# A two-block transformer forward pass in fp32: seams between stages rearranged, with rooms of their own for two splits, square root tables loaded ahead, and weight splits placed beside the tile reads that free them

## The reference, cut to what matters

```python
# first block
h = rmsnorm(x, norm_mix_g); p, q, k, v = split(h @ w_in)
pool_out = multiscale_pool(p); attn_out = diff_attention(rope(q), rope(k), v)
x = x + concat(pool_out, attn_out) @ w_o                       # stages proj1, wo
u = causal_dwconv(rmsnorm(x, norm_ffn_g) @ w_up)               # up1, 5632 wide
gate, val = split(u); x = x + (silu(gate) * val) @ w_down      # down1
x = rmsnorm(x, norm_final_g)
# second block
h = h + 0.5 * rms_norm(swiglu(rms_norm(h, ffn1_pre_g)), ffn1_post_g)      # up2, down2
u = rms_norm(h, mix_pre_g); proj = u @ w_in                               # proj2
y_a = sparse_latent_attention(proj); y_b = rms_norm(hgrn2(proj)) * silu(g_h)
merged = sigmoid(gate_a + b_gate[:D]) * (y_a @ w_br_a) \
       + sigmoid(gate_b + b_gate[D:]) * (y_b @ w_br_b)                    # branch
h = h + rms_norm(merged @ w_out, mix_post_g)                              # out
h = h + 0.5 * rms_norm(swiglu(rms_norm(h, ffn2_pre_g)), ffn2_post_g)      # up3, down3
ple_gate = sigmoid(rms_norm(h, ple_pre_g) @ w_ple_gate)                   # ple
h = h + rms_norm(ple_gate * (p @ w_ple_proj), ple_post_g)                 # pproj
```

## Time and profile before

| | |
|---|---|
| median of 3 runs | 2042.51 us (2041.75 to 2043.58) |
| profiled execution | 2042.38 us |
| its span | 2040.6 us |
| PE busy | 1855.1 us, 91% |
| DVE busy | 1169.4 us, 57% |
| ACT busy | 648.9 us, 32% |
| POOL busy | 201.3 us, 10% |
| DMA | 180.61 MB, mean 89 GB/s |

### The profile page before, as it was taken

One profiled execution on the slowest core, in us unless ns is written; L12 is line 12 of the kernel. 1 busy time (PEld: TensorE's weight loads), 2 busy tenths in 40 slices (PEclk: granted clock), 3 DMA queues, 4 the chain that ended last, 5 costly groups with the idle time before them and its releaser, 6 DMA issues.

```text
span 2040.6 us, 23459 instructions
## 1 busy us (share of the span) xinstructions
PE 1855.1 (91%) x8230; PEld 1481.6 (73%) x8230; DVE 1169.4 (57%) x1775; ACT 648.9 (32%) x954; POOL 201.3 (10%) x150
## 2 busy tenths in 40 slices
PE   5987999999999999999899989867778999999986
PEld 4665777777887888888677766656556788888864
DVE  6447568888534655532534786577663755552256
ACT  4333322222223222222323335443443422222243
POOL 2221000000000000000033344243000000000000
PEclk9888999999999999999899999978899999999988
DMA  3421222223322222332222332311242232232212
GB/s 136 82 67 38 83 73 93 93 93 104 100 95 78 86 100 95 98 112 95 67 83 73 121 127 63 131 40 32 72 134 83 73 103 93 96 118 96 91 50 74
DMA packets 55340, 180.61 MB, mean 89 GB/s; under 512 B 6216, under 2 KB 6984, under 8 KB 55272
## 3 DMA queue, kind: packets, MB, share of 16 engines
q1 hardware_dynamic: 43200, 157.07, 23.3%
q10 hardware_dynamic: 12072, 22.67, 4.0%
HBM read 167.65 MB, written 12.06 MB: 88 GB/s over the span
## 4 chain that ended last, share of the span: by engine, by line
PE 68%; DVE 20%; issue 6%; DMA 3%; ACT 2%; DVEq 1%; POOL 1%; ACTq 0%; SPq 0%; POOLq 0%
PE bank L713 17%; PE bank L715 16%; PE bank L714 16%; PE bank L735 2%; PE bank L736 2%; PE bank L737 2%; PE bank L794 2%; PE bank L795 2%; PE bank L796 2%; DMA raw<-in_w_proj 1%; DVE sq L1930 1%; PE bank L774 1%; DVE chunk L1751 1%; PE bank L1063 1%; DVE score L2079 1%
## 5 line engine op out<-in xcount | busy, mean ns | idle before, releaser
L1124 ACT ACTIVATE w_hi<-raw 128x1024 fp32r<-128x1024 f32 (+2 forms) x281 | 305.3, 1088 | 787.8 <-PE bank L715 703.3
L713 PE MATMUL bank<-a_hi,w_hi 128*128 128x512 f32 x1312 | 520.4, 397 | 25.2 <-DVE w_lo L1658 17.4
L714 PE MATMUL bank<-a_lo,w_hi 128*128 128x512 f32 x1312 | 513.7, 392 | 0.0
L715 PE MATMUL bank<-a_hi,w_lo 128*128 128x512 f32 x1312 | 513.6, 391 | 0.0
L1658 DVE TENSOR_TENSOR w_lo<-raw,w_hi 128x1024 fp32r<-128x1024 f32 (+2 forms) x219 | 279.7, 1281 | 267.1 <-ACT w_hi L1124 257.9
L713 PEld LDWEIGHTS bank<-a_hi,w_hi 128*128 128x128 f32 x1312 | 247.8, 189 | 96.0 <-issue 25.1
L715 PEld LDWEIGHTS bank<-a_hi,w_lo 128*128 128x128 f32 x1312 | 248.0, 189 | 52.4
L714 PEld LDWEIGHTS bank<-a_lo,w_hi 128*128 128x128 f32 x1312 | 248.1, 189 | 51.4 <-issue 1.0
L625 POOL TENSOR_TENSOR w_lo<-raw,w_hi 128x1024 fp32r<-128x1024 f32 x54 | 130.0, 2410 | 1106.6 <-ACT w_hi L1124 1106.6
L714 PE MATMUL bank<-h_lo,w_hi 128*128 128x512 f32 x568 | 221.1, 389 | 0.0
L715 PE MATMUL bank<-h_hi,w_lo 128*128 128x512 f32 x568 | 221.1, 389 | 0.0
(11 more groups left out here) (272 smaller groups left out, 2155.5 us busy)
## 6 DMA issues: line engine op xcount, KB each, us to landing
raw<-in_w_up SPq DMA_DIRECT2D x132, 512.0 KB, 3.3
...
```

The costliest lines, as they stand in the source:

```text
L713: mm(dst[:, :], wh, hi[:, k, :], start=(first and c == 0), stop=False)
L714: mm(dst[:, :], wh, lo[:, k, :], start=False, stop=False)
L715: step = mm(dst[:, :], wl, hi[:, k, :], start=False, stop=(last and c == n - 1))
L1124: fn(w_hi[:, slot, 0:size], raw[:, slot, 0:size], ACT.Copy).then_inc(unit_high, 1)
```

## The change

1. **Rooms.** wo's input gets its own `mix_hi` and `mix_lo`, so that `a_hi` and `a_lo` are free while wo runs. The split of x for up1 is made inside wo's tile loop, by ACT and by DVE. `sum_x("norm2")` moves from ahead of up1's first three tiles to behind them. pproj's input gets `p_split`.
2. **Root tables.** `load_root_table()`, a square root of one column, stands in ACT's queue at six places: at the end of the attention, after up2's silus, ahead of the branch stage, ahead of out, after up3's silus, and behind the last sigmoid of ple.
3. **Last square on PE.** For post1, postmix and plepost PE sums the sum of seven squares, then the eighth square onto it (16 products of one column), and DVE doesn't add the eighth.
4. **`add_branch`.** The first chunk takes its factor from PSUM, and the copy to `rstd` comes after the first `x`. `units` places two splits of ple's units within it.
5. **End.** post2's sum goes ahead of pproj's third tile and its spread ahead of the fifth; ACT's root, high parts, copies of pproj and split for ple are interleaved.
6. **Up stages.** In up1, up2 and up3 the split of unit 5 stands one tile earlier (up1: at the read of tile 1; up2 and up3: behind the first `val`).
7. **Branch.** The split of the unit that takes a tile's slot stands right behind the tile's read, no longer both behind `h_lo`.

The core of the diff:

```diff
             def sum_x(name):
+                stat_bank_free(name)
+                if name in LAST_ON_PE:
+                    q = square_at(name, DC - 1)
+                    pe.wait_ge(sum_added, q)
+                    sum_columns(sum_sq, stop=False)
+                    pe.wait_ge(sq_ready, q + 1)
+                    sum_columns(sq[:, q % 2, :], start=False).then_inc(total_ready, 1)
+                    return
                 pe.wait_ge(sum_added, square_at(name, DC - 1) + 1)
-                stat_bank_free(name)
                 sum_columns(sum_sq).then_inc(total_ready, 1)
 
...
-            first_three("wo", "mix1", spread_after=(1, 2, 3, 4))
+            first_three("wo", "mix1", mix_hi, mix_lo, spread_after=(1, 2, 3, 4))
             for i in range(3, DC):
-                project("wo", i)
-            hidden("up1", "norm2", AUX["pool", len(WINDOWS) - 1] + 1, summed=True)
+                project("wo", i, None, mix_hi, mix_lo)
+            hidden("up1", "norm2", AUX["pool", len(WINDOWS) - 1] + 1)
...
             for i in range(DC):
                 dst, u = tile_bank("pproj", i), UNIT["pproj"][0] + i // 4
+                if i == 2:
+                    sum_x("post2")
+                if i == 4:
+                    spread("post2")
...
+            def load_root_table():
+                fn(small[:, 60:61], prm("eps"), ACT.Sqrt)
...
                 if a == ATT_STEPS:
-                    highs("mix1", 0, 4)
+                    load_root_table()
+                    highs("mix1", 0, 4, mix_hi)
             unit_high_part(UNIT["wo"][0] + 3)
             take_root("head", P, HEADS * QB)
-            highs("mix1", 4, 4)
+            highs("mix1", 4, 4, mix_hi)
             for k in range(DC):
                 if k == DC - 1:
                     last_tile_finished("wo")
                 else:
                     tile_finished("wo", k)
+                wait(tile_read("wo", k))
+                scaled_high("norm_ffn_g", k)
                 square("norm2", k, x[:, k, :], tile_read("wo", k))
             unit_high_part(UNIT["up1"][0] + 3)
-            for k in range(DC):
-                scaled_high("norm_ffn_g", k)
             take_root("norm2", D)
...
             silus("up2", 1)
+            load_root_table()
             keep_branch("down2", "post1")
             take_root("post1", D)
...
             load_gates(1)
 
+            load_root_table()
             for t in range(4):
                 act.wait_ge(chunk_ready, SPLIT["y"] + t + 1)
                 fn(a_hi[:, t, :], ya[:, t, :], ACT.Copy).then_inc(hi_ready, 1)
...
             unit_high_part(UNIT["out"][0] + 3)
+            load_root_table()
             keep_branch("out", "postmix")
             take_root("postmix", D)
             scaled_highs("pre2", "ffn2_pre_g", 2 * DC, "up3")
             silus("up3", 2)
+            load_root_table()
 
             for c in range(2):
                 act.dma_start(pe_in[:, c, :], ins["pt"][c]).then_inc(p_loaded, 16)
-            highs("p", 0, 2)
+            highs("p", 0, 2, p_split)
             keep_branch("down3", "post2")
-            for i in range(DC):
+
+            def keep_pproj(i):
+
                 if i % 4 == 3:
                     units_done(UNIT["pproj"][0] + i // 4 + 1)
                 else:
                     act.wait_ge(head_ready, 2 * HEADS + DSA_HEADS + i - i // 4 + 1)
                 fn(p_proj[:, i, :], tile_bank("pproj", i)[:, :], ACT.Copy).then_inc(tile_sem("pproj", i), 1)
+
+            keep_pproj(0)
+            keep_pproj(1)
             take_root("post2", D)
-            scaled_highs("plepre", "ple_pre_g", 3 * DC, "ple")
+            unit_high_part(UNIT["ple"][0] + 1)
+            for i in (2, 3, 4):
+                keep_pproj(i)
+            for k in range(DC):
+                act.wait_ge(x_ready, 3 * DC + k + 1)
+                scaled_high("ple_pre_g", k)
+                if k < 3:
+                    keep_pproj(5 + k)
+                square("plepre", k, x[:, k, :], (x_ready, 3 * DC + k + 1))
+                if k < 2:
+                    unit_high_part(UNIT["ple"][0] + 2 + k)
+            take_root("plepre", D)
+            for n in range(2):
+                units_done(UNIT["ple"][0] + n + 1)
...
+                if i == DC - 1:
+                    load_root_table()
                 if i:
                     square("plepost", i - 1, p_proj[:, i - 1, :], (y_ready, i))
             take_root("plepost", D)
...
@@ -1739,23 +1794,30 @@
                         add_square(folded_to, k)
                     late_splits(stage, k)
 
-            def add_branch(name, g, src, last_read, signal, before, square_stage=None, split=None):
-
-                rsqrt(name)
+            def add_branch(name, g, src, last_read, signal, before, square_stage=None, split=None, units={}):
+
+                invert(name)
+                make_diagonal()
+                dve.wait_ge(spread_ready, STAT[name] + 1)
                 for k in range(DC + 1):
                     if k < DC:
                         if last_read is not None:
                             wait(last_read(k))
                         if k >= 2:
                             dve.wait_ge(signal, before + k - 1)
-                        step(v.scalar_tensor_tensor(chunk[:, k % 2, :], src[:, k, :], prm(g, k), rstd[:, :],
+                        factor = rstd if k else stat_bank
+                        step(v.scalar_tensor_tensor(chunk[:, k % 2, :], src[:, k, :], prm(g, k), factor[:, :],
                                                     ALU.mult, ALU.mult))
                         v.tensor_tensor(x[:, k, :], x[:, k, :], chunk[:, k % 2, :], ALU.add).then_inc(signal, 1)
+                    if k == 0:
+                        take_rstd(name)
                     if k and square_stage:
                         add_square(square_stage, k - 1)
                     if k and split:
                         scaled_low(split[0], split[1], k - 1)
                         add_square(split[0], k - 1)
+                    if k in units:
+                        split_unit(units[k])
...
                         dve.wait_ge(tile_sem("up1", tile), TILE["up1", tile][1] + 1 + it)
                         if i >= skip:
                             split_unit(first + 4 * turn + i + 3, it, 4)
+                        if skip and i == 1:
+                            split_unit(first + 5)
...
                         v.tensor_tensor(val[:, :], bank[u][:, :], rstd[:, :], ALU.mult).then_inc(bank_free[u], 1)
                         dve.wait_ge(bank_free[u], u_uses + 1 + it)
+                        if skip and j == 0:
+                            split_unit(u0 + 5)
...
-                    add_square(square_stage, k)
+                    if k < DC - 1 or square_stage not in LAST_ON_PE:
+                        add_square(square_stage, k)
...
                     wait(tile_read("branch", 2 * m + n))
+                    if m or n:
+                        split_unit(UNIT["branch"][0] + 2 * m + n + 3)
                 slot_free(c)
                 v.tensor_tensor(chunk[:, c % 2, :], gated[:, 0, :], gated[:, 1, :], ALU.add).then_inc(
                     chunk_ready, 1)
@@ -2270,8 +2337,6 @@
                     scale_gates(m + 1)
                 made(c)
                 low(c, h_lo[:, m, :], h_hi[:, m, :])
-                for u in (2 * m + 3, 2 * m + 4) if m else (4,):
-                    split_unit(UNIT["branch"][0] + u)
...
             branch_kept("down3", "post2")
-            for i in (1, 2):
-                split_unit(UNIT["ple"][0] + i)
             add_branch("post2", "ffn2_post_g", y, lambda k: tile_read("down3", k), x_ready, 3 * DC,
-                       split=("plepre", "ple_pre_g"))
+                       split=("plepre", "ple_pre_g"), units={0: UNIT["ple"][0] + 1, 2: UNIT["ple"][0] + 2})
```

60 lines of the change are left out of this document (36 added, 24 removed).

## The result

The changed kernel takes **2029.26 us** (median of 4 runs, 2027.11 to 2031.31) against 2043.05 (4 runs, 2041.75 to 2044.62): a ratio of 0.9933, 95% interval 0.9921 to 0.9945. It is faster by 13.8 us, where 20.6 was forecast, and lies just above the range. Its profiled execution is the slowest of the four, 2031.31 us with a span of 2029.4, so the two profiles differ by 11.2 us only.

A forecast was written before the change was run, and what follows sets the result against it. TensorE, busy 1855.1 of 2040.6 us, bounds the kernel; gains come only from 174 us idle and low-clock stretches. Terms sum to 20.6 us, taking the profiled 2042.4 to 2021.8 us, range 2015.5 to 2029.

The forecast's parts named there:

- the seam from wo to up1: End of wo to up1's first three tiles: they end 2.4 us earlier, bounds 1 and 3.5.
- the last seam: Behind ple: new table load delays the square and TensorE sums twice, a loss of 0.7 us, bounds -1.6 and +0.7.
- The branch stage's period: Branch stage: pairs of tiles 6.0 us apart instead of 7.09; with an earlier start +7.9 us, bounds 2.6 and 9.0.
- the table load ahead of it: Ahead of the branch stage: root table load and dummy root delay the high parts of ya, a loss of 1.5 us.
- the two seams with the eighth square on TensorE: Seams of down2 (post1) and out (postmix): one add saved, spread perhaps at full clock, +1.3 us each.
- pproj and ple: The end: post2's sum and spread hidden within pproj, ple starts 4.8 us earlier, +6.5 us in all.
- I take it to go with the gap: 1.7 more: up2, unit 5: half-clock stretch vanishes with the 1.86 us wait, adding 1.7 for +3.4 us; bounds 1.7 and 3.5.
- Rival 1: Branch stage: gates keep the period near 7.09 us, only the earlier start is won, 2.6 for 7.9; 2027 us, chance 0.15.
- rival 3: Table loads on the path stop their queue for twice their 1.28 us row, 2.6 us more; 2024.4 us, chance 0.08.
- the slower one: Up stages: early split of unit 5 shifts their phase, the 1.86 us wait returns each round; 2062 us, chance 0.02.
- Rival 5: Waits only move to the next unit in up2, and at the end; 2028 us, chance 0.08.
- Rival 2: Seams do better than bounded: full-clock spreads, wo's seam, hidden load, no last-seam loss, 4.3 us more; 2017.5 us, chance 0.22.

The follow-up runs named there:

- experiment 1: Changed kernel with mix_lo, the low part of wo's input, moved up by 32 bytes: 2026.02 us, ratio 0.9926.
- experiments 2 and 3: Kernel before with a_lo 32 bytes higher: 2061.34 us; changed kernel with mix_lo or mix_hi moved: 2027.91, 2028.48 us; both moved, plus up1's early low part: 2019.65 us.
- experiment 4: Changed kernel with mix_lo 96 bytes up and the low part of up1's unit 2 made before the wait for wo's last tile: 2020.22 us.
- experiment 6: Changed kernel with plepost's root table load and second sum undone: 2026.79 us; with only the second sum undone: 2025.53 us.
- experiment 8: Changed kernel with unit 5's split and high part in up2 and up3 back where they were: 2027.14 us.

## Why the prediction was wrong

**What failed.** Two terms of the sum were mis-sized, the seam from wo to up1 (0.3 for +2.4) and the last seam (-2.8 for -0.7), and the stretches between the seams were put at nothing, where they took 3.5 us back in this profile. Of the 20.6 forecast the two profiles show 11.2; these three make up 7.7 of the 9.4 that are missing, small parts the rest.

**Direction and most terms held.** The branch stage's period (5.95 for the 6.0 forecast), its gain (7.4 for 7.9), the table load ahead of it (-1.4 for -1.5), the two seams with the eighth square on TensorE (0.9 each for 1.3; the spreads stayed at half clock in this profile), pproj and ple (6.2 for 6.5; ple starts 17.24 us after pproj for 21.70, 4.5 for the 4.8 forecast) and the zeros of up1, up3, down3 and of the other loads came as worked out. In other runs the spread of one of the two seams ran at full clock (1.12 us in experiment 1's) and its seam took 9.13 for 10.96 before, a gain of 1.8, the upper bound. The table load at the attention's end (192.6 to 193.9 us) lies in ScalarE's wait for VectorE, which lasts to 195.9.

**"wo to up1: +2.4" gave 0.3.** The start of up1's tiles was right, 1.8 of the 2.0. What was not seen is that a room of its own has a place of its own: wo went from 0.680 to 0.700 us for three matmuls, -0.9 (experiments 2 and 3). I had checked what the new rooms overlap and not how fast they are read. Then, the stretch at half clock that began in the gap reached further into up1's first tiles (to 263.2, 5.8 us in, for 261.4, 4.9 us in), and they took 18.9 us for 18.5, where I had counted on 0.4 less. And the term asked which chain ends the wait, but not whether its last member had to stand there: it didn't, and 3.7 us lay in it (experiment 4).

**"The last seam: -0.7" was -2.8.** The wait for the squares grew by 0.2, where next to nothing was forecast, but the sums cost 3.55 us for 1.05: sixteen products at half clock. The term that was mis-sized is the second sum, which I had costed at 0.95, from the row of before, which happened to fall into full clock. The load costs 0.9 of the 2.8, the second sum 1.0, and 0.8 is the first sum at half clock (experiment 6). Even by its own terms, a start 0.03 later and 0.95 more of sum, the forecast would have been -1.0 and not -0.7.

**The clock, and one execution.** up2's "I take it to go with the gap: 1.7 more" came out (3.3 for 3.4) by luck: with the gap there the stretch stayed away in two executions of three (experiment 8). The edit is worth 1.7 and not 3.4; the profiled execution of before had a stretch there by chance. Stretches that were put at nothing show how large such chance is: over the runs based on the changed kernel start to wo's first took 195.9 to 198.8 us in a profile, and proj2 to the wait ahead of the branch stage 434.7 to 440.8, and here they took 3.5 of the gain back (1.8 and 1.7). Not all of that is the clock: 0.7 of the 1.8 were there before TensorE's first matmul (19.40 us for 18.68), and how the rest divides is not shown. I had set a sum of single seams against one execution as if the rest stood still. The 174 us of idle time that the prediction starts from are 185.5 by the earlier trace rows; no term was worked out from them.

**The range** of 2015.5 to 2029.0 took in each rival alone but not three terms short at once. Rival 1 (the gates bind), rival 3 (a load that costs twice its row) and the slower one are refuted: 5.95, 1.37 and 2029.26. Rival 5 (the wait moves to the next unit in up2 and at the end as well) did not come: no such wait is left in up2, and the end gained 6.2. In up1 it does move, as forecast, for the earlier trace rows:

```profile
295.97 0.50 PE L721 MATMUL bank<-a_hi,w_hi 128*128 128x512 f32 x1 [1.12 <-DVE w_lo L1711]
```

TensorE waits one unit later, 1.12 for 3.10, and the stage is no shorter. Rival 2 (all seams at their best) did not come either.

**Open.** Why the place of an operand sets its pace, with which period, and why 0.695 and 0.700 both occur with the same places. Whether the half clock ahead of a given tile can be steered: filled idle time took it away behind out's start in three runs out of three, but a wait of 1.8 to 1.9 in up2 was followed by either clock, and one of 4.2 to 4.3 ahead of the last sum by a sum of 1.05 or of 1.84.
